# The combine of a retrieval layer: when gathered rows are added, and which engine squares the output

## What is computed

```python
def peer_ffn(h, w_q, sub_keys, u_experts, v_experts):
    ...
    act = jax.nn.gelu(jnp.einsum('cd,chkd->chk', xc, u_experts[ic]).astype(F32), approximate=False)
    wgt = (gc * act).astype(xc.dtype)
    return jnp.einsum('chk,chkd->cd', wgt, v_experts[ic])
...
return x + gate2 * peer_ffn(...)      # then rmsnorm(x, g_final)
```

## Time and profile before

| | |
|---|---|
| median of 3 runs | 1932.87 us (1932.79 to 1933.21) |
| the profiled execution | 1940.21 us |
| its span | 1938.3 us |
| TensorE, matmuls | 1838.3 us busy, 95% |
| VectorE | 1514.0 us busy, 78% |
| GpSimd | 757.5 us busy, 39% |
| ScalarE | 726.8 us busy, 37% |
| DMA | 526.21 MB, mean 271 GB/s |

### The profile page before, as it was taken

One profiled execution on the slowest core, in us unless ns is written; L12 is line 12 of the kernel. 1 busy time (PEld: TensorE's weight loads), 2 busy tenths in 40 slices (PEclk: granted clock), 3 DMA queues, 4 the chain that ended last, 5 costly groups with the idle time before them and its releaser, 6 DMA issues. The chain is left out here.

```text
span 1938.3 us, 26856 instructions
## 1 busy us (share of the span) xinstructions
PE 1838.3 (95%) x9796; PEld 1614.6 (83%) x9796; DVE 1514.0 (78%) x2279; ACT 726.8 (37%) x969; POOL 757.5 (39%) x485
## 2 busy tenths in 40 slices
PE   5999979999899899999999999999889999999997
PEld 5888857777788887998999999999868888888886
DVE  7666367775446678888878989999778988988888
ACT  3322234443423322333333356666532333333331
POOL 0000097000032000667777868888343333344330
PEclk9999989999999999999999999999999999999999
DMA  8899278879494071679999979999999999999992
GB/s 307 279 326 327 88 184 229 253 224 259 140 291 132 4 153 23 168 197 256 271 259 289 277 252 350 339 362 349 330 387 388 389 390 389 389 388 390 386 362 83
DMA packets 304053, 526.21 MB, mean 271 GB/s; under 512 B 19130, under 2 KB 209131, under 8 KB 299372
## 3 DMA queue, kind: packets, MB, share of 16 engines
q1 hardware_dynamic: 246444, 371.17, 59.1%
q0 software_dynamic: 36864, 134.23, 20.0%
q10 hardware_dynamic: 20672, 19.93, 4.9%
HBM read 438.75 MB, written 85.99 MB: 271 GB/s over the span
## 5 line engine op out<-in xcount | busy, mean ns | idle before, releaser
L125 PE MATMUL u_s<-h_hi,u_hi 128*128 128x384 f32 x1024 | 353.9, 346 | 16.4 <-POOL u_lo L1964 12.7
L126 PE MATMUL u_s<-h_lo,u_hi 128*128 128x384 f32 x1024 | 348.1, 340 | 0.0
L127 PE MATMUL u_s<-h_hi,u_lo 128*128 128x384 f32 x1024 | 347.5, 339 | 0.0
L125 PE MATMUL v_o<-v_v_hi,v_w_hi 128*128 128x512 f32 x768 | 300.6, 391 | 13.0 <-DVE v_w_lo L2218 7.2
L126 PE MATMUL v_o<-v_v_lo,v_w_hi 128*128 128x512 f32 x768 | 300.0, 391 | 0.0
L127 PE MATMUL v_o<-v_v_hi,v_w_lo 128*128 128x512 f32 x768 | 299.8, 390 | 0.0
L1964 POOL TENSOR_TENSOR u_lo<-u_ut,u_hi 128x1024 fp32r<-128x1024 f32 x79 | 195.5, 2474 | 76.4 <-ACT u_hi L1738 74.9
L125 PEld LDWEIGHTS u_s<-h_hi,u_hi 128*128 128x128 f32 x1024 | 196.5, 192 | 20.4 <-issue 13.0
L126 PEld LDWEIGHTS u_s<-h_lo,u_hi 128*128 128x128 f32 x1024 | 196.6, 192 | 0.0
L127 PEld LDWEIGHTS u_s<-h_hi,u_lo 128*128 128x128 f32 x1024 | 196.0, 191 | 0.0
L1397 POOL DMA_INDIRECT rows_buf<-in_u_experts_dram,few_idx x117 | 159.2, 1361 | 84.9 <-DMA v_gt<-expert_gates 57.8
(11 more groups left out here) (344 smaller groups left out, 3977.9 us busy)
## 6 DMA issues: line engine op xcount, KB each, us to landing
v_raw<-in_v_experts_dram SPq DMA_DIRECT2D x74, 512.0 KB
v_slot<-in_v_experts_dram SPq DMA_DIRECT2D x54, 512.0 KB
expert_acts<-u_ao SPq DMA_DIRECT2D x64, 384.0 KB
u_raw<-turned_experts SPq DMA_DIRECT2D x24, 1024.0 KB, 6.4
expert_gates<-u_gs SPq DMA_DIRECT2D x12, 2048.0 KB
v_gt<-expert_gates SPq DMA_DIRECT2D x30, 768.0 KB
u_raw<-in_u_experts_dram SPq DMA_DIRECT2D x84, 256.0 KB
u_raw<-in_u_experts_dram ACTq DMA_DIRECT2D x76, 256.0 KB
```

What stands on the lines that cost most here:

```text
L125: nc.tensor.matmul(out, w[0], x[0], start=first, stop=False)
L126: nc.tensor.matmul(out, w[0], x[1], start=False, stop=False)
L127: return nc.tensor.matmul(out, w[1], x[0], start=False, stop=last)
```

## The change

`late_by` and `adds_by` start from group 2 (`ROWS_FROM`) and all rows are dealt by group 30 (`ROWS_TO`), so none are added in groups 1, 2 and 31. The late ones end with group 18 (`LATE_BY`). `total` no longer squares: it signals `sum_ok`, ScalarE runs an ACTIVATE with the function Square and an accumulated sum (`squares`), signals `sq_ok`, and VectorE goes on with `moments`. The last lines of VectorE are reordered: each tile's `finish` follows its own `moments`, except the third's, which comes after the sums of the last tile.

```diff
--- before.py
+++ after.py
@@ -1601,7 +1601,8 @@
 NSLOT = PH * TOPK
 LATE = 20
 SOON = NSLOT - LATE
-LATE_BY = 16
+LATE_BY = 18
+ROWS_FROM, ROWS_TO = 2, NE // P // GT - 2
 
 
 def dots_by(t):
@@ -2040,12 +2041,12 @@
 
 def late_by(g):
 
-    return LATE * min(g, LATE_BY) // LATE_BY
+    return LATE * max(0, min(g, LATE_BY) - ROWS_FROM) // (LATE_BY - ROWS_FROM)
 
 
 def adds_by(g):
 
-    return (NSLOT + LATE) * g // (NE // P // GT - 1) - late_by(g)
+    return (NSLOT + LATE) * max(0, min(g, ROWS_TO) - ROWS_FROM) // (ROWS_TO - ROWS_FROM) - late_by(g)
 
 
 def late_slot(n):
@@ -2082,7 +2083,7 @@
         p_o = [k.ps(f"o{i}", [P, D]) for i in range(DT)]
         p_a = k.ps("a", [P, D])
         names = ("w_in1 gt_in0 gt_in1 wl0_ok w0_ok hi0_ok gf_in vhi_ok vlo_ok w_ok whi_ok wlo_ok mm "
-                 "ssq_ok root_ok y_ok out_ok dg_ok wg_ok add_ok").split()
+                 "sum_ok sq_ok ssq_ok root_ok y_ok out_ok dg_ok wg_ok add_ok").split()
         sem = {n: k.sem(n) for n in names}
         row_in = [k.sem(f"row_in{j}") for j in range(VRING)]
         dve_c = k.count("dve_chain")
@@ -2188,7 +2189,16 @@
             for g in range(LATE_BY + 2, NG):
                 split(g)
                 weights(g)
+            def squares(n, i, cs, to):
+                act.wait_ge(sem["sum_ok"], n)
+                nc.scalar.activation(sq[:, cs], acc[:, i, cs], ACT.Square, accum_out=to).then_inc(sem["sq_ok"], 1)
+
             for i in range(TT):
+                if i < TT - 1:
+                    squares(i + 1, i, slice(0, D), ssq[:, i:i + 1])
+                else:
+                    for h in range(2):
+                        squares(TT + h, i, slice(h * S, (h + 1) * S), halves[:, h:h + 1])
                 act.wait_ge(sem["ssq_ok"], 2 * i + 2)
                 r = root[:, i:i + 1]
                 nc.scalar.activation(r, r, ACT.Sqrt, bias=keep["eps"][:, :], scale=DOWN / D).then_inc(sem["root_ok"], 1)
@@ -2270,13 +2280,14 @@
                     nc.vector.tensor_tensor(few["wg"][:, SOON:], few["dots"][:, SOON:], sel[:, 2, 0, SOON:], ALU.mult).then_inc(sem["wg_ok"], 1)
                     dve.wait_ge(sem["wg_ok"], 2)
 
-            def total(i, bank):
-
-                chained(dve, dve_c, nc.vector.tensor_tensor(acc[:, i, :], bank, gate2[:, :], ALU.mult))
-                chained(dve, dve_c, nc.vector.tensor_tensor(acc[:, i, :], acc[:, i, :], x2[:, i, :], ALU.add))
-                chained(dve, dve_c, nc.vector.tensor_tensor_reduce(
-                    out=sq[:, :], in0=acc[:, i, :], in1=acc[:, i, :], scale=1.0, scalar=0.0,
-                    op0=ALU.mult, op1=ALU.add, accum_out=ssq[:, i:i + 1]))
+            def total(i, bank, cs=slice(0, D)):
+
+                chained(dve, dve_c, nc.vector.tensor_tensor(acc[:, i, cs], bank[:, cs], gate2[:, cs], ALU.mult))
+                nc.vector.tensor_tensor(acc[:, i, cs], acc[:, i, cs], x2[:, i, cs], ALU.add).then_inc(sem["sum_ok"], 1)
+
+            def moments(i):
+
+                dve.wait_ge(sem["sq_ok"], i + 1)
                 rstd_dve_in(nc, sem["ssq_ok"], ssq[:, i:i + 1], fin[:, i:i + 1], root[:, i:i + 1])
 
             def finish(i):
@@ -2285,25 +2296,26 @@
                 rstd_dve_out(nc, dve, dve_c, root[:, i:i + 1], fin[:, i:i + 1])
                 nc.vector.scalar_tensor_tensor(acc[:, i, :], acc[:, i, :], root[:, i:i + 1], g_fin[:, :], ALU.mult, ALU.mult).then_inc(sem["y_ok"], 1)
 
+            last = TT - 1
+            done = 2 * DT * (NG - 1)
             dve.wait_ge(sem["gf_in"], 32)
             dve.wait_ge(sem["add_ok"], NSLOT + LATE)
-            total(0, p_a[:, :])
-            for i in range(DT - 1):
-
-                dve.wait_ge(sem["mm"], 2 * DT * (NG - 1) + 2 * i + 2)
-                total(i + 1, p_o[i][:, :])
-                finish(i)
-            last = TT - 1
-            for h in range(2):
-                cs = slice(h * S, (h + 1) * S)
-                dve.wait_ge(sem["mm"], 2 * DT * NG - 1 + h)
-                chained(dve, dve_c, nc.vector.tensor_tensor(acc[:, last, cs], p_o[DT - 1][:, cs], gate2[:, cs], ALU.mult))
-                chained(dve, dve_c, nc.vector.tensor_tensor(acc[:, last, cs], acc[:, last, cs], x2[:, last, cs], ALU.add))
-                chained(dve, dve_c, nc.vector.tensor_tensor_reduce(
-                    out=sq[:, cs], in0=acc[:, last, cs], in1=acc[:, last, cs], scale=1.0, scalar=0.0,
-                    op0=ALU.mult, op1=ALU.add, accum_out=halves[:, h:h + 1]))
-                if h == 0:
-                    finish(last - 1)
+            total(0, p_a)
+            moments(0)
+            finish(0)
+            dve.wait_ge(sem["mm"], done + 2)
+            total(1, p_o[0])
+            moments(1)
+            finish(1)
+            dve.wait_ge(sem["mm"], done + 4)
+            total(2, p_o[1])
+            dve.wait_ge(sem["mm"], done + 5)
+            total(last, p_o[2], slice(0, S))
+            moments(2)
+            dve.wait_ge(sem["mm"], done + 6)
+            total(last, p_o[2], slice(S, D))
+            finish(2)
+            dve.wait_ge(sem["sq_ok"], TT + 1)
             chained(dve, dve_c, nc.vector.tensor_tensor(ssq[:, last:TT], halves[:, 0:1], halves[:, 1:2], ALU.add))
             rstd_dve_in(nc, sem["ssq_ok"], ssq[:, last:TT], fin[:, last:TT], root[:, last:TT])
             dve.wait_ge(sem["root_ok"], TT)
```

## The result

| | before | after |
|---|---|---|
| median beside each other, us | 1933.04 (1932.79 to 1934.69, 4 runs) | 1917.76 (1916.22 to 1921.12, 4 runs) |
| ratio | 1 | 0.9929 [0.991, 0.9949] |
| span of the profiled execution, us | 1938.3 | 1914.6 |
| combine stage begins (ScalarE's first high part of the values) | 1390.47 | 1376.54 |
| combine stage, from there to the end of the span | 547.83 | 538.06 |

The kernel became faster, by 15.3 us of the medians where 9.7 were forecast, and the time lies 2.7 us under the range given. Of the 23.7 us between the two spans only 9.8 lie in the combine, the one stage that the change touches. The other 13.9 were there before it began, in stages whose code is the same in both.

What follows compares the result with a forecast made beforehand. TensorE's matmul stream was taken to bound the combine, with DMA-caused gaps in the first groups and VectorE late in the tail. -8.3 + 1.5 - 2.9 = -9.7 us: profiled 1940.21 to 1930.5, less 7.34, 1923.2; range 1920.5 to 1928.5.

Steps and rivals of the forecast that it cites:

- Part 1: Start of the combine: without rows in groups 1 and 2, group 3's values land earlier and TensorE's gaps go, 8.3 us gained.
- Part 2: Groups 4 to 30: denser rows leave the DMA short by 0.24 us per group; 1.5 us lost, bounds 0 and 6.4.
- the cushion: Slack from a group's fourth tile to the next group, to pay the DMA shortage: 3.9 us at group 6, -1.9 at 27.
- Rival B: DMA bounds from group 3 on, so all 6.4 us are given back: 1928.1 to 1929.6 us; chance 0.17.
- Part 3: After the last matmuls: Squares on ScalarE and reordered VectorE work end the tail sooner, 2.9 us gained, bounds 2.0 and 3.1.
- Rival E: Tail on ScalarE: root and square need different tables, loads of 1.28 us, 2.6 less gain, 1925.8 us; chance 0.02.
- C: Gap before group 3 stays, caused by the tile's place in SyncE's queue: only the tail won, 1930.0 us; chance 0.10.
- D: Groups 12 to 30: VectorE falls behind, slots free late, DMA idles between; 12 us slower, 1945; chance 0.05.
- the differences lie in stages that the profile slows alike: Outside the combine: the profiled execution's 7.34 us over the median of 1932.87 carried over, turning 1930.5 into 1923.2.

Runs made afterwards that it cites:

- half additions: The kernel with only the new tail, VectorE adding half of each gathered row, transfers unchanged: 1926.3 us, one run; gap before group 3 5.73 us.
- half rows: The kernel with only the new tail, VectorE's additions halved and 128 values rows gathered at half width: 1917.8 us, one run; gap before group 3 1.26 us.
- the run from group 7 on: The changed kernel with the rows packed into groups 7 to 30, 6.17 per group: 1932.28 us, ratio 1.0021.
- before again: The kernel before, unchanged, run against itself: 1932.08 us (12 runs) against 1929.91 (29 runs), ratio 1.0002.
- rows 1 to 30: The changed kernel with the rows dealt over groups 1 to 30, 4.93 per group: 1927.03 us, ratio 0.9992.
- tail only: The kernel before with only the new tail, its rows dealt as before: 1925.64 us, ratio 0.9981.
- rows only: The kernel before with only the tables that deal the rows changed, its tail as before: 1923.28 us, ratio 0.9965.
- rows 3 to 31: The changed kernel with the rows running on to group 31, six of them in it: 1917.52 us, ratio 0.9936.
- the change again: The changed kernel, unchanged, profiled and timed a second time: 1919.99 us, ratio 0.9933.
- two rows in the last: The changed kernel with two rows left for group 31 and the first tile's moments behind the second tile's sums: 1916.18 us, ratio 0.993.

## Why the prediction was right, and where it was wrong

**Part 1 was right in mechanism, place and size.** The stretch of matmuls fell by 6.63 us where 8.3 less 1.5, 6.8, was forecast. The gap before group 3 went with its low clock, and so did group 2's. Group 1's was still there (0.91 by the earlier trace rows, now 0.75); of it only 0.2 had been counted, and other profiles with rows from group 3 lack it. That the bytes did it is shown by half additions against half rows, one profile of each.

**Part 2 was right.** The late gaps are 1.21 and 0.54 us with the pitch taken off, 1.75 for the 1.5 taken, ahead of groups 27 and 30; the cushion was to end at about 22. One of them, 1.04 us of idle time, is just over the 1 us that the prediction allowed. Rival B (all 6.4 us given back) had the right cause and the wrong size. The cushion counted from the earlier trace rows was there. The Trainium skill, DMA: Bandwidth & Descriptors, section Where 436 GB/s comes from, has the HBM side bind at about 358 GB/s. The trace after does not agree either: 391 GB/s for 360 us, by a program on one core.

**Part 3 was right**, 3.15 us for 2.9, just over its bound of 3.1. The Square took 1.06 + 0.18 us for the estimate's 1.14 + 0.19, and 0.61 + 0.19 for the half. Rival E is gone: Squares and roots alternate after a single load at 1893.11, under group 31's matmuls. The Trainium skill, ScalarE: Activation LUTs, section Table sets: the hidden batching unit, whose entry for the root's set names no square (nor all that the set holds), leaves more loads possible; this trace has one.

**C and D.** C fell with the half rows and with both kernels that deal from group 3. D was right as a place where such a change turns slower, as the run from group 7 on shows, but by idle DMA engines early rather than by a VectorE that falls behind.

**What failed is the sentence "the differences lie in stages that the profile slows alike, so I carry them over: 1923.2", and the range with it.** The combine's gain was forecast to 0.1 us (9.7 for 9.8; 10.6 as a mean of two profiles of each). But the prediction took the three runs of before for its time, and put what the stages ahead of the combine do from one execution to the next at nothing. The runs put a size to it: in the 14 profiles the combine begins between 1374.33 and 1390.47 us, both ends being the kernel before, and the kernel before had medians of 1933.04, 1929.91 and 1930.28 in three comparisons (and 1928.61 in a single run). That these stages took 13.9 us less in the one profile, and 5.5 less in the medians (15.3 less the combine's 9.8), was not forecast, and with it the time fell out of the range. What decides on the change itself is whether time follows the combine. It does, in the same order over all eight kernels with more than one run, though the intervals of neighbours overlap:

| kernel | combine, us | ratio to before [95%] |
|---|---|---|
| rows from group 7 | 551.98 | 1.0021 [1.0009, 1.0034] |
| before again | 549.07 | 1.0002 [0.9985, 1.0018] |
| rows 1 to 30 | 545.74 | 0.9992 [0.9979, 1.0005] |
| tail only | 544.90 | 0.9981 [0.9963, 0.9998] |
| rows only | 542.31 | 0.9965 [0.9947, 0.9983] |
| rows 3 to 31 | 537.90 | 0.9936 [0.9921, 0.9951] |
| the change again | 537.70 | 0.9933 [0.9907, 0.9959] |
| two rows in the last | 536.69 | 0.9930 [0.9917, 0.9943] |

From first to last the combine shortens by 15.3 us and the time by 0.0091 x 1930 = 17.6 us. The change's own 11.4 us there (549.07 to 537.70) stand against 12.9 of time by its ratio, with an interval from 7.9 to 17.9; in medians, 9.9. So the change is worth 10 to 13 us, of which the combine accounts for 10 to 11; the first comparison's 15.3 probably had a few us of luck in it. Its ratio's interval starts at 9.9 us, just beyond the 9.7 forecast. Whether the four kernels with the shortest combines also have some 2 us more ahead of it is open: their intervals reach the combine's own gain or nearly so, and the profiles of kernels that gain little or nothing begin the combine as early as any: before again (1374.33), rows from group 7 (1376.12), tail only (1377.10).

## What to carry to other kernels

Ask of a gap that ends with an engine's instruction how many bytes stand ahead of the tile that it waited for; here, moving them out of the first two groups paid, and moving them out of six left the DMA engines partly idle while the slots were full, and came back as gaps later. Compare two versions by the stage that differs, with both ends read from the trace: a span or a handful of runs mixes it with what the rest of the program does from one execution to the next, and here that was larger than the change. And a range for a time needs, beside the bounds of the mechanism, the spread of repeated runs, which three runs 0.4 us apart need not show.

## What the runs showed of the hardware that was not expected

- The same program on the same data ran between 1922.69 and 1943.75 us (29 runs, one core). Of the 16.1 us between the two profiles of before, 5.1 arise in the stage of the mixing, where TensorE waits 5.0 us in one and not in the other, and most of the rest in the expert stage, where its granted clock falls to 0.77 for stretches of 15 us in one and does not fall under 0.89 in the other; the combine repeats within 0.4 us for the change (538.06, 537.70) and 1.2 for before (547.83, 549.07). What sets off either was not tried.
- Halving the rows' transfers (their number the same) took the DMA share from 1.05 to 0.91 and the rate from 391 to 316 GB/s in the late groups, and the late gaps were gone.
- The table load of 1.28 us ahead of the first root cost nothing where VectorE came to the first tile 16.7 us ahead of the last matmul, and was on the path where it came 14.2 ahead. In the last run's order, which puts the second tile's sums between, the tail was the short one at 13.9 too.
